# A fifth landing buffer for weights, laid over tiles of the first two blocks, used from the first mixer on

## The reference, cut to what matters

```
x = first_block(...)            # DEPTH = 2 blocks: 18 projections, five branches, 5 gates of 1024x1024, w_out
mix = nsa_moba_mixer(x)         # "first mixer": x @ ab_w_in, attention, @ ab_w_out
x = layer_norm(a*x + mix); x = layer_norm(a*x + hierarchical_moe(x))
mix = stick_breaking_mixer(x)   # "second mixer": x @ sb_w_in, attention, @ sb_w_out
x = layer_norm(a*x + mix); x = layer_norm(a*x + hierarchical_moe(x))
```

## Time and profile before

| what | us |
|---|---|
| time, median of 3 runs | 1416.14 (1416.07 to 1417.88) |
| the profiled execution's own time | 1407.65 |
| its span, first to last instruction | 1405.9 |
| TensorE matmuls busy | 1343.5 (96%) |
| VectorE busy | 1086.8 (77%) |
| ScalarE busy | 605.9 (43%) |
| the 16 DMA engines' queue q1, share of the span | 48.7% |

### The profile page before, as it was taken

One profiled execution on the slowest core, in us unless ns is written; L12 is line 12 of the kernel. 1 busy time (PEld: TensorE's weight loads), 2 busy tenths in 40 slices (PEclk: granted clock), 3 DMA queues, 4 the chain that ended last, 5 costly groups with the idle time before them and its releaser, 6 DMA issues.

```text
span 1405.9 us, 22646 instructions
## 1 busy us (share of the span) xinstructions
PE 1343.5 (96%) x9134; PEld 1207.7 (86%) x9134; DVE 1086.8 (77%) x1410; ACT 605.9 (43%) x877; POOL 61.2 (4%) x90
## 2 busy tenths in 40 slices
PE   7999999998999999999999999999989988999997
PEld 6999888996999998998897788888789867988876
DVE  7788797667987898658878886777876588668777
ACT  4543432334333332333314644656641382456663
POOL 1110100003000000000201300000000000000000
PEclk9999999999999999999999999999999999999999
DMA  8554744544454543552653043788945504278792
GB/s 263 160 165 151 249 146 140 175 150 135 150 163 155 199 146 120 169 189 90 210 182 119 15 166 131 266 288 279 317 156 180 180 1 150 102 276 300 264 313 94
DMA packets 194999, 249.65 MB, mean 178 GB/s; under 512 B 5786, under 2 KB 168858, under 8 KB 194896
## 3 DMA queue, kind: packets, MB, share of 16 engines
q1 hardware_dynamic: 189136, 227.66, 48.7%
q0 software_dynamic: 5072, 18.73, 3.7%
q10 hardware_dynamic: 688, 1.82, 0.3%
HBM read 246.09 MB, written 2.10 MB: 177 GB/s over the span
## 4 chain that ended last, share of the span: by engine, by line
PE 76%; DVE 15%; ACT 4%; issue 2%; DMA 1%; POOL 1%; SPq 0%; DVEq 0%; ACTq 0%; POOLq 0%
PE bank L483 37%; PE bank L507 8%; PE bank L1039 7%; PE bank L1095 5%; PE bank L701 4%; DVE wL L1899 4%; PE bank L1076 3%; PE bank L533 2%; DVE wH L1897 2%; DVE proj L2069 1%; PE bank L581 1%; DMA ring<-in_moe_w_up 1%; PE bank L1117 1%; DVE X L2325 1%; ACT proj L1867 1%
## 5 line engine op out<-in xcount | busy, mean ns | idle before, releaser
L483 PE MATMUL bank<-hH,wL 128*128 128x256 f32 x1744 | 493.2, 283 | 0.0
L483 PE MATMUL bank<-hH,wH 128*128 128x256 f32 x1680 | 485.8, 289 | 7.5 <-DVE wL L1899 7.5
L483 PE MATMUL bank<-hL,wH 128*128 128x256 f32 x1680 | 475.1, 283 | 0.0
L1899 DVE TENSOR_TENSOR wL<-ring,wH 128x2048 fp32r<-128x2048 f32 x175 | 400.9, 2292 | 56.6 <-ACT wH L1753 39.3
L483 PEld LDWEIGHTS bank<-hH,wH 128*128 128x128 f32 x1680 | 321.7, 192 | 16.6 <-DVE wL L1899 11.0
L483 PEld LDWEIGHTS bank<-hH,wL 128*128 128x128 f32 x1744 | 334.1, 192 | 0.0
L483 PEld LDWEIGHTS bank<-hL,wH 128*128 128x128 f32 x1680 | 322.0, 192 | 1.3 <-issue 0.2
L1753 ACT ACTIVATE wH<-ring 128x2048 fp32r<-128x2048 f32 x59 | 113.2, 1919 | 38.0 <-DMA ring<-in_moe_w_up 26.3
L1897 DVE CAST wH<-ring 128x2048 fp32r<-128x2048 f32 x68 | 83.5, 1228 | 17.6 <-PE bank L483 13.0
L1478 ACT ACTIVATE big<-bank 128x512 f32<-128x512 f32 x40 | 23.9, 598 | 148.3 <-PE bank L483 148.2
L507 PE MATMUL bank<-wH,hH 128*128 128x512 f32 x176 | 69.9, 397 | 0.1
(11 more groups left out here) (463 smaller groups left out, 2257.7 us busy)
## 6 DMA issues: line engine op xcount, KB each, us to landing
ring<-in_w_gate SPq DMA_DIRECT2D x40, 1024.0 KB, 5.0
ring<-in_w_in SPq DMA_DIRECT2D x34, 1024.0 KB, 5.3
ring<-in_moe_w_down SPq DMA_DIRECT2D x26, 1024.0 KB, 5.7
ring<-in_moe_w_gate SPq DMA_DIRECT2D x32, 512.0 KB, 4.3
ring<-in_moe_w_up SPq DMA_DIRECT2D x32, 512.0 KB, 5.4
ring<-in_moe_w_gate SPq DMA_DIRECT2D x12, 1024.0 KB, 5.3
ring<-in_sb_w_in SPq DMA_DIRECT2D x12, 1024.0 KB, 5.0
ring<-in_ab_w_in SPq DMA_DIRECT2D x11, 1024.0 KB, 4.9
```

The source lines that it names most:

```text
L483: last = mm(ps[:, m * CW:m * CW + (width if token_major else S)], a, b, start=k == 0 and i == 0, stop=k == KT - 1 and i == 2)
L1899: tt(low, raw_w, high, ALU.subtract).then_inc(split_ready, 1)
```

## The change

Two tiles, `late_raw` (float32) and `late_low` (float32r), are laid at one address over HV, AV, MV, `convs` and part of `scw`, which only the first two blocks use; `scw` is declared earlier so that it lies there too, and the tiles declared between its two places (L, PT, hsR, the constants) move by its size. The new buffer, LATE, has no user until the program of TensorE has written out the last block's output projection; there its "previous user" is set to the end of that projection's first column half. From then on `new_chunk` may always take LATE: five landing buffers instead of four outside the expert stages, six instead of five inside them. The high tiles, the order of the chunks and the instructions of PE, ACT, DVE and POOL stay as they are.

```
-        def beneath(*named):
+        def beneath(*named, dt=F32):
...
-            places = [nc.sbuf_tensor(name, shape, F32) for name, shape in named]
+            places = [nc.sbuf_tensor(name, shape, dt) for name, shape in named]
...
+        late_raw, = beneath(("late_raw", [P, KT * CW]))
+        late_low, = beneath(("late_low", [P, KT * CW]), dt=F32R)
         HV = sb("HV", [P, T, W])
         AV = sb("AV", [P, T, 2 * HD])
         MV = sb("MV", [P, T, W])
         convs = sb("convs", [P, CT, S + CONF_K - 1])
+        scw = sb("scw", [P, CT, S + SC_K - 1])
...
-        landed = [sem(f"chunk{i}_landed") for i in range(RING + 1)]
+        landed = [sem(f"chunk{i}_landed") for i in range(RING + 2)]
...
-        SPARE, GATE_HIGH = RING, HIGHS + 1
-        raw_user, raw_order = [None] * (RING + 1), list(range(RING + 1))
+        SPARE, LATE, GATE_HIGH = RING, RING + 1, HIGHS + 1
+        raw_user, raw_order = [None] * (RING + 2), list(range(RING + 2))
...
-            slot = oldest(raw_order, range(RING + 1 if spare else RING))
+            slot = oldest(raw_order, [*range(RING), *([SPARE] if spare else []), *([LATE] if raw_user[LATE] else [])])
...
-            return ring[:, raw_slot[i], :] if raw_slot[i] < RING else work[:, 0:KT * CW]
+            return ring[:, raw_slot[i], :] if raw_slot[i] < RING else late_raw[:, :] if raw_slot[i] == LATE else work[:, 0:KT * CW]
...
-            return wL[:, raw_slot[i], :] if raw_slot[i] < RING else XHL[:, 0, :]
+            return wL[:, raw_slot[i], :] if raw_slot[i] < RING else late_low[:, :] if raw_slot[i] == LATE else XHL[:, 0, :]
...
+            raw_user[LATE] = ("out", DEPTH - 1, 0, T - 1)
             if stop == "block1":
                 return
```

More of the change, by code:

```diff
@@ L135, in build @@
         sct = L[:, 0, :, :].rearrange("p c n -> p (c n)")
-        scw = sb("scw", [P, CT, S + SC_K - 1])
         relrow = sb("relrow", [P, AT_HEADS])
@@ L335, in next_chunk @@
             i = len(chunks)
-            slot = new_chunk(parts, last_item, None, CW, False)
+            new_chunk(parts, last_item, None, CW, False)
             pe.wait_ge(*landed_at(i))
-            return ring[:, slot, :]
+            return raw_tile(i)
         def next_split(pe, parts, last_item, width=CW, spare=(False, False), scalar=False, alone=False):
```

## The result

| | before | after |
|---|---|---|
| median us, 20 runs of each, taken together | 1412.70 (1406.35 to 1417.88) | 1402.82 (1401.04 to 1407.83) |
| the profiled execution's own time | 1407.65 | 1407.47 |
| its span | 1405.9 | 1405.7 |
| TensorE matmuls busy | 1343.5 | 1347.1 |

The ratio is 0.9940, with a 95% interval from 0.9924 to 0.9955: 6.4 to 10.7 us less than 1412.70. The change makes the kernel faster, by 0.6%. The forecast was a gain of 6.4 us and a time of 1409.7, within 1405.5 to 1416.6.

A forecast was written before the change was run, and what follows sets the result against it. TensorE was taken to bound the kernel, waiting at turns 14 for loads issued late for want of a free buffer. Gains 3.87 + 2.52 = 6.4 us; 1407.65 - 6.4 = 1401.3, plus 8.5 gives 1409.7; range 1405.5 to 1416.6.

The forecast's parts named there:

- margins: First expert stage, turn 14: f1(14) ready with 0.8 us to spare, f2(14) idle 0 to 0.2 us, taken as 0.
- the addresses: Moved addresses of L, PT, hsR and the constants: change no instruction, so 0 us.
- the other stages' loads: Loads of other stages start one chunk earlier behind a PE that did not wait: 0 us.
- the first mixer's chunk 0: Start of first mixer: load hidden by 0.7 us, cost taken as 0, between 0 and 5.3 us.
- L485: Waits of 2.2 us before this line, L483 before the change: not touched, gain 0, at most 2.2 us.
- the DMA share in the 7 us: Sign in the changed kernel's trace: DMA share in the 7 us before the late landing should be near 0.9.
- Rival B: Turns 14: ACT's or DVE's order binds next, gain 2.5 to 5.2 us, about 1412.5; chance 0.14.
- C: Sparse stretch: bytes bind, stalls stay, gain 0 to 1 us, 1415.6; chance 0.17.
- D: First mixer's chunk 0, first SPARE chunks: loads share bandwidth evenly, cost 7.8 us, nothing gained, 1423.9; chance 0.07.
- the term of 8.5 us: Whole kernel: median of the runs, 1416.14, lies 8.5 us above the profiled execution; added to 1401.3.
- the clock: Twelve matmuls behind the first stage's stall: 4.62 us becomes 2.75; nothing counted behind the second stage's stall.
- the idle time: TensorE's waits before L1039 in both turns 14 go: 2.00 us in the first stage, 2.05 + 0.47 in the second.

The follow-up runs named there:

- e4: Changed kernel, but f1(14) and f2(14) of both expert stages wait for the chunks they waited for before the change; 1412.32 us, ratio to before 1.0000.
- e2: Changed kernel, but the new buffer is handed out only outside the expert stages; 1414.49 us, ratio to before 1.0013.
- e1: Changed kernel's memory layout, but the new buffer never gets a user and is never handed out; 1411.46 us, ratio to before 0.9998.
- e10: The changed kernel without edit, run again beside the kernel before; 1405.60 us, ratio to before 0.9957.
- e8: Changed kernel, but f2(14) alone waits as before the change, for f1(13), in both expert stages; 1405.52 us, ratio to before 0.9961.
- e9: The kernel before without edit, run again for a second profile and its spread; 1413.08 us, ratio to before 1.0014.

## Why the prediction was right in kind and wrong in its number

**What held.** The place, the mechanism and the order of steps, each as forecast. f1(14) and f2(14) of the two turns 14 are the whole gain: e4 undoes it by four waits and e2 gets none of it without them. f1(14) issued 0.74 us behind f1(12) (forecast 0.73); its cast directly behind the copy L1832; margins of 0.59 and 0.41 us where the forecast had 0.8 and 0 to 0.2 of idle; matmuls at 2.75. The costs put at nothing were nothing that shows: the addresses (e1), the other stages' loads (e2, e4), the first mixer's chunk 0 (670.40 as before, with 0.33 us of slack left), L485. One sign failed: the DMA share in the 7 us was 0.76 and not near 0.9.

**What was luck in it.** f1(14) landed later than the forecast allowed, about 6.3 us after the second part's issue and not 4.76. Crowded engines don't account for it: from 1002.00 to 1003.50, up to 0.4 us before that landing, their share was 0.06. Nearly all of the bytes were there, and what held back the last of them no run here shows. It cost nothing because ACT's cast was bound by L1832 anyway. Rival B, ACT's and DVE's order, missed by these 0.4 to 0.6 us. C, that the bytes bind, is refuted: the stalls went, and with a share of 0.76 there was time to spare in the engines. (The prediction took 354 GB/s for their full rate; its own row of 1362.40 to 1364.60 has 406.) Of D, later landings did show (6.3 for 4.76 at f1(14), 6 for 5.2 at chunk 0), and both ran into cover. At D's own place, the first chunk in SPARE in turn 2, the subtraction ended at 879.60 + 2.29 = 881.89 and TensorE started at 881.94, 0.2 to 0.3 us behind its pace of one matmul in 0.12:

```profile
879.60 2.29 DVE L1902 TENSOR_TENSOR XHL<-work,XHL 128x2048 fp32r<-128x2048 f32 x1 [7.52 <-ACT XHL L1756]
...
881.50 0.28 PE L485 MATMUL bank<-hL,wH 128*128 128x256 f32 x1
881.62 0.28 PE L485 MATMUL bank<-hH,wL 128*128 128x256 f32 x1
881.94 0.39 PE L485 MATMUL bank<-hH,XHL 128*128 128x256 f32 x1
```

Neither the second stage nor e10's first shows that, so a later landing cost at most 0.3 us here, where D had feared 3.0 twice.

**The step that failed: "The median of the runs, 1416.14, lies 8.5 above that execution; the same difference gives 1409.7".** That median was of 3 runs. Over 20 it is 1412.70, 3.4 us lower, and runs of this kernel lie between 1406.35 and 1417.88. The three happened to lie near the top. Of the 1409.7 - 1402.82 = 6.9 us by which I missed, 3.4 are this: the term of 8.5 us measured 1412.70 - 1407.65 = 5.05, and 4.2 against the mean of 99 further runs, 1411.9. The sign was right, because the profiled execution was a cheap one: its clock cost it 12.7 us ((1 - 0.991) x 1405.9), where the kernels with both stalls lose 17.5 in the table above. The range was built around the same anchor and went with it; for the scatter of executions it had one stretch at the lower clock at the bottom and "a little more" at the top. From 1412.70 the same terms give 1406.3, and the same range, moved with it, would have begun at 1402.1 and held 1402.82.

**The second term that was mis-sized: the clock.** I counted one stretch (1.87 us, first stage) and gave the second stall none, from one execution where it had none. The row that I named for it in the earlier trace rows is of the stall itself; this is the one behind it, with a clock of 1.00 as well:

```profile
1364.60:1369.20 4.60, 4.12 (x18) 3.20 (x19) 4.00 (x5) 4.47 (x5) 0.00 (x0) 1.00 1.08 356
```

Whether a stall is followed by the low clock is a matter of the execution: 11 of 16. On average both stalls together cost 2.4 ± 1.1 us by the clock, which does not exclude 1.87; that the way of counting was wrong is shown, its size is not. **The third: the idle time**, 4.5 us in the forecast; the rest fell by 1394.6 - 1389.4 = 5.2 ± 0.6 us. Together 7.6 us (the difference of the means 1412.1 and 1404.5, ± 0.8) instead of 6.4; e10's ratio alone gives 6.1. So the gain was undersized by about 1.2 ± 0.8 us, and what is left of the miss, 6.9 - 3.4 - 1.2 = 2.3 us, is the scatter of medians of 20 runs: over more runs of the two kernels (99 and 32) the means lie at 1411.9 and 1404.3, 7.6 apart, where the two medians are 9.9 apart.

**What stays open.** The clock's cost in the kernels with one stall, 18.7 ± 1.7, is above that of both (17.5 ± 0.6), and e8's, 12.9 ± 1.6, below that of none (15.1 ± 0.9); the count of stretches predicts 16.4 and 15.1. Both stay unexplained. Of the 0.7 us between 4.5 and 5.2, the interval of ± 0.6 and the rough split between clock and rest can hold nearly all.

## What to carry to other kernels

A stall that appears at one place of a repeating schedule is first a question of eligibility: list for each load how many chunks back its release lies, and look at the one that breaks the pattern; a rule that lets it use the buffer that is already there may be worth as much as a new buffer. Take the time before from many runs, or from the mean granted clock of each, before adding a difference of a few microseconds to it; the profiled execution may differ from the median by more than the change is worth. When two chunks in a row are late, cost the second as if the first were cured.

## What the runs showed of the hardware that I had not expected

An idle stretch of TensorE of about 2 us was followed by 3.4 us at the lower clock level in 9 of 14 cases, and one of 4.6 or 4.8 us in 2 of 2, in the same program at the same place in one execution and not in another; after two of 1.34 and 1.35 us it was not, and without a stall there was none at these places. The profiled executions also had such stretches, of 3.4 or 6.8 us, around 346, 825, 1046 and 1183 us (within some 10 us) and at the end, some of them at other places too, and their length varied between executions of one program: 3.4 us at 824.5 in one execution of before, 6.8 at 826.5 in another (e9). The cost of all of them together, about 15 us in a kernel without the two stalls, is twice the gain of this change. The scatter of ±0.4% between runs is for the most part this clock: the 111 runs of before whose clock is on record lie between 1405.67 and 1418.23 with the mean granted clock between 0.983 and 0.992, and in 99 of them the correlation of the time with the clock's cost is 0.89. And a load can end long after its bulk: f1(14) landed near 1003.9, though the engines' share was 0.06 from 1002.00 to 1003.50.
